# Constant products in TensorE's norm waits: six, one, four and two of them become none

## What is computed

```python
def rms_norm(t, gain):
    t32 = t.astype(jnp.float32)
    y = t32 * lax.rsqrt(jnp.mean(t32 * t32, axis=-1, keepdims=True) + NORM_EPS)
    return (y * gain.astype(jnp.float32)).astype(t.dtype)

# first block
x = (x + gt1 * rms_norm(mix_out, norm_mix_post[l])).astype(x.dtype)
h = rms_norm(x, norm_ffn_pre[l]) * (1.0 + sc2) + sh2
f = jnp.square(jax.nn.relu(h @ w_ff1[l])) @ w_ff2[l]
x = (x + gt2 * rms_norm(f, norm_ffn_post[l])).astype(x.dtype)
# hybrid layer
h = rms_norm_2(x, g_mix)
proj = h @ w_in
...
g = jax.nn.sigmoid(rms_norm_2(x, g_ple_in) @ w_ple_gate)
return x + g * e
```

## Time and profile before

| | |
|---|---|
| median of 3 runs | 3424.12 us (3423.11 to 3424.27) |
| profiled execution | 3424.06 us, span 3422.1 us |
| TensorE products, busy | 3238.1 us, 95% of the span |
| TensorE weight loads, busy | 2564.4 us, 75% |
| VectorE, ScalarE, GpSimd, busy | 1995.4, 1066.0, 1673.5 us |
| granted TensorE clock, mean | 0.98 of full speed |
| moved by DMA | 268.37 MB, mean 78 GB/s |

### The profile page before, as it was taken

How to read it: one execution, slowest core, us unless ns; L and a number is a source line. 1 busy time by engine, 2 the same in 40 slices (tenths; PEclk the granted TensorE clock), 3 DMA queues, 4 the chain that set the end, 5 groups by cost and what they waited for, 6 DMA issues and landing times.

```text
span 3422.1 us, 52681 instructions
## 1 busy us (share of the span) xinstructions
PE 3238.1 (95%) x19342; PEld 2564.4 (75%) x19342; DVE 1995.4 (58%) x2743; ACT 1066.0 (31%) x1986; POOL 1673.5 (49%) x1323
## 2 busy tenths in 40 slices
PE   7988999999999999899999999999989999999999
PEld 4766777777888887577777788877657777787887
DVE  5556677755566556524645666656552735586466
ACT  2142433432111113543443311112551535231112
POOL 3423323225476664144444666655226263566665
PEclk9998999999999999899999999999999999999999
DMA  5431111112233222012122222322012121223232
GB/s 208 154 136 45 45 38 43 40 32 79 91 98 98 96 88 68 26 62 68 56 68 63 86 98 92 98 80 86 31 38 93 44 82 49 81 93 98 92 98 93
DMA packets 71658, 268.37 MB, mean 78 GB/s; under 512 B 7840, under 2 KB 7968, under 8 KB 68384
## 3 DMA queue, kind: packets, MB, share of 16 engines
q1 hardware_dynamic: 69152, 260.73, 23.0%
q10 hardware_dynamic: 2304, 4.83, 0.4%
HBM read 263.44 MB, written 2.10 MB: 78 GB/s over the span
## 4 chain that ended last, share of the span: by engine, by line
PE 77%; DVE 16%; ACT 4%; issue 2%; DMA 1%; POOL 0%; SPq 0%; DVEq 0%; ACTq 0%; POOLq 0%
PE psum_a L574 10%; PE psum_a L578 10%; PE psum_a L577 10%; PE psum_d L574 5%; PE psum_d L578 5%; PE psum_d L577 5%; PE psum_d L637 4%; PE psum_a L729 3%; PE psum_d L832 2%; PE psum_a L600 2%; PE psum_a L603 2%; PE psum_a L604 2%; PE psum_a L759 1%; PE psum_a L763 1%; PE psum_a L762 1%
## 5 line engine op out<-in xcount | busy, mean ns | idle before, releaser
L3306 POOL TENSOR_TENSOR w_lo<-raw,w_hi 128x1024 fp32r<-128x1024 f32 x440 | 1114.4, 2533 | 36.7
L3302 POOL TENSOR_TENSOR mark<-mark 128x1 f32<-128x1 f32 x438 | 104.9, 240 | 1672.4 <-PE psum_a L574 838.1
L574 PE MATMUL psum_a<-h_hi,w_hi 128*128 128x512 f32 x1712 | 676.0, 395 | 0.0
L578 PE MATMUL psum_a<-h_hi,w_lo 128*128 128x512 f32 x1712 | 668.3, 390 | 0.0
L577 PE MATMUL psum_a<-h_lo,w_hi 128*128 128x512 f32 x1712 | 668.0, 390 | 0.0
L3303 POOL TENSOR_SCALAR w_hi<-raw 128x1024 fp32r<-128x1024 f32 x440 | 471.2, 1071 | 33.8 <-DMA raw<-in_weights 33.8
L574 PEld LDWEIGHTS psum_a<-h_hi,w_hi 128*128 128x128 f32 x1712 | 322.7, 189 | 77.7 <-issue 11.2
L577 PEld LDWEIGHTS psum_a<-h_lo,w_hi 128*128 128x128 f32 x1712 | 322.6, 188 | 67.6 <-issue 1.9
L578 PEld LDWEIGHTS psum_a<-h_hi,w_lo 128*128 128x128 f32 x1712 | 322.3, 188 | 67.9
L574 PE MATMUL psum_d<-split,w_hi 128*128 128x512 f32 x848 | 331.1, 390 | 9.6 <-DVE x L3053 6.8
L577 PE MATMUL psum_d<-split,w_hi 128*128 128x512 f32 x848 | 330.0, 389 | 0.0
(11 more groups left out here) (396 smaller groups left out, 5702.1 us busy)
## 6 DMA issues: line engine op xcount, KB each, us to landing
raw<-in_weights SPq DMA_DIRECT2D x440, 512.0 KB, 3.4
plain<-in_ada SPq DMA_DIRECT2D x20, 1024.0 KB, 6.9
arena<-in_ada SPq DMA_DIRECT2D x4, 1024.0 KB, 17.5
x<-in_x SPq DMA_DIRECT2D x1, 2048.0 KB, 12.8
x<-in_x ACTq DMA_DIRECT2D x1, 2048.0 KB, 10.7
out<-x SPq DMA_DIRECT2D x8, 256.0 KB, 3.7
arena<-in_pe ACTq DMA_DIRECT2D x2, 512.0 KB, 4.4
const<-in_const ACTq DMA_DIRECT2D x1, 906.0 KB, 9.3
```

The lines of the kernel that those rows point to most:

```text
L574: m = pe.eng.matmul(dst, wh, hi(t), start=t == 0, stop=False)
L578: m = pe.eng.matmul(dst, wl, hi(t), start=False, stop=t == k - 1)
L3302: eng.tensor_tensor(b.mark[:, 1:2], b.mark[:, 0:1], b.mark[:, 0:1], ALU.add)
L3306: eng.tensor_tensor(lo, b.raw[:, s], hi.bitcast(F32), ALU.subtract).then_inc(sig["w_ready"], 1)
```

## The change

One line of constants. All calls of pe_unused and the loop in pe_norm_direct stay, with zero products each; so does the wait on free_a in pe_unused and the wait on free_d in pe_norm_direct. Every other instruction of every engine stays as it was.

```diff
@@ -668,7 +668,7 @@
         pe.eng.matmul(pe.b.psum["a"][:, n0 % BANKS, 0:2 * P], pe.b.ident, pe.b.const[:, C_MASK4:C_MASK4 + 2 * P], start=True, stop=True)
 
 
-UNUSED = (6, 1, 4, 2)
+UNUSED = (0, 0, 0, 0)
 
 
 def pe_norm(pe, N):
```

## The result

The changed kernel takes 3439.6 us (median of 5), the kernel before 3423.45 us beside it: 16.2 us more, ratio 1.0047 with a 95% interval of 1.0037 to 1.0058. The profiled execution took 3441.41 us, 17.35 more than that of before; it is the longest of the five.

A forecast was written before the change was run, and what follows sets the result against it. TensorE bounds the kernel (77% of the chain), with short waits for norms. Low-clock terms of 4.4, 3.5, 2.3, 1.2 and 3.3 us over five stretches give 14.7, so 3424.1 + 14.7 = 3438.8 us, range 3429 to 3447.

The forecast's parts named there:

- A: 899 to 924 us, pe_norm then pe_norm_direct: spread 0.8, turns 0.4, last spread 0.9, restart 2.3, together 4.4 us slower.
- B: 1273 to 1299 us, pe_norm then pe_norm_direct: spread 0.8, turns 0.4, restart 2.3, together 3.5 us slower.
- C: 2293 to 2306 us, pe_norm alone: sums and spread already at the low clock, so only the restart, 2.3 us slower.
- D: 2350 to 2365 us, pe_norm alone: restart 2.3, less 0.5 already low, less 0.6 for products in the way: 1.2 slower.
- E: 3362 to 3373 us, pe_norm alone: sums +0.9, spread +0.7, restart 2.3, less 0.6: 3.3 us slower.
- restart: Full product stream behind each norm begins at half rate, low for 4.7 us on average: 2.3 us lost each, 1.6 to 2.9.
- waits and turns: Sums, spreads and direct turns ahead of the products: low clock adds up to 0.9 per spread or sums, 0.4 for turns.
- Direct turns: Sums in pe_norm_direct, A and B: 1.66 to 1.75 us a turn at low clock, now 1.757; net +0.4, between -0.8 and +0.7.
- Rival 1: The clock keeps its level in A, turns at 1.51 us, only gains are left: 3419.4 us, chance 0.06.
- Rival 2: Low restarts behind each norm are hidden by VectorE and ScalarE splitting h, only 3.7 us stay: 3427.8 us, chance 0.09.
- Rival 3: Low level costs half its whole length, 67 us more low in the five stretches, 33.5 lost: 3457.6 us, chance 0.03.
- The allowance for the moment: Some twelve later unfilled waits meet the clock's changes at other moments, a microsecond or two each either way, together about 3.

The follow-up runs named there:

- e1: Kernel before without the two constant products of each direct turn, the other constant products kept: 3427.36 against 3422.9 us, +4.5, ratio 1.0014.
- e3: Kernel before without the four constant products behind each spread, the others kept: 3456.16 against 3422.9 us, +33.3, ratio 1.0104.
- e4: Kernel before with one constant product in each direct turn in place of two: 3429.86 against 3422.9 us, +7.0, ratio 1.0027.
- e8: Changed kernel with the two products of each direct turn put back: 3461.04 us against 3423.5 for the kernel before, +37.5, ratio 1.0114.
- e7: Changed kernel with the four products behind each spread put back: 3427.65 us against 3423.5 for the kernel before, +4.2, ratio 1.0015.
- The two shifts: Kernel before with eight, then four, constant products added once ahead of A's norm: 3426.37 against 3423.5 us (+2.9), and 3426.17 against 3422.7 (+3.5).
- e2: Kernel before without the six constant products ahead of the first sums, the others kept: 3427.49 against 3422.9 us, +4.6, ratio 1.0016.

## Why the prediction was right, step by step

**The direction and the mechanism held.** The removed products gave back nothing where they had stood in waits, and the clock fell in the first waits of A and B. The forecast of 3438.8 us stands against 3439.6, +14.7 against +16.2.

**The single terms, from the profiled executions.** A weight load that both kernels have stands later in the changed kernel by what was lost up to there. The lag is 0.0 us ahead of A and 5.4 behind it, 10.1 behind B, 10.2 ahead of C and 13.1 behind it, 14.7 behind D, 13.8 ahead of E and 17.5 behind it. For A the load behind the restart, before and after (931.90 + 5.42 = 937.32):

```profile
931.90 0.19 PEld L603 LDWEIGHTS psum_a<-h_lo,w_hi 128*128 128x128 f32 x1
...
937.32 0.19 PEld L603 LDWEIGHTS psum_a<-h_lo,w_hi 128*128 128x128 f32 x1
```

The first L600 of each stretch divides its loss into waits and turns ahead of it and the restart behind it:

| stretch | waits and turns, forecast | measured | restart, forecast | measured | sum, forecast | measured |
|---|---|---|---|---|---|---|
| A | 2.1 | 2.6 | 2.3 | 2.8 | 4.4 | 5.4 |
| B | 1.2 | 2.1 | 2.3 | 2.6 | 3.5 | 4.7 |
| C | 0 | 0.1 | 2.3 | 2.8 | 2.3 | 2.9 |
| D | -0.6 | -0.4 | 1.8 | 2.0 | 1.2 | 1.6 |
| E | 1.0 | 1.1 | 2.3 | 2.6 | 3.3 | 3.7 |

The sum is 18.3 us where 14.7 were forecast, so every term was too small, the restarts by 1.8 us together and the waits and turns by 1.8. The restart was sized by the mean of five of the old kernel, 4.7 us low; the five that came were low for 6.0, 5.6, 6.0, 5.4 and 5.7. Two of the five that were averaged (3.2 and 3.4 us) were shorter than any that came. In the waits it is above all B: its last spread was taken as low already, and the rest as in A, but 0.9 us more were lost.

**What made up for it.** The span grew by 17.5 us and not by 18.3, because of low stretches outside the norms. The kernel before has one of 3.4 us, among products that run without a gap:

```profile
2397.20:2400.40 3.20, 3.20 (x9) 2.49 (x8) 0.20 (x1) 0.28 (x2) 2.99 (x3) 0.50 0.00 0
```

The changed kernel has 1.00 over the same work (the window from 2405 to 2420 us above), and the lag falls from 14.7 to 13.1 us there. Against it, a low stretch that was 6.8 us long from 2513 on is 10.2 us long in the changed kernel and costs 0.8 us. The start of that work, before and after:

```profile
2510.50:2513.10 2.60, 1.11 (x8) 0.29 (x8) 1.19 (x3) 0.00 (x0) 0.00 (x0) 1.00 0.62 205
...
2523.60:2526.20 2.60, 2.04 (x8) 0.44 (x8) 0.37 (x2) 0.00 (x0) 0.00 (x0) 0.50 0.58 205
```

In sum these later low stretches kept their length, as the forecast's last sign asks, and each cost or gave what stood in it. The forecast had allowed some 3 us for such changes without saying which way. The terms were 3.6 us too small; 0.8 us of that was taken back outside the norms, and the median of the changed kernel lies 1.8 us under its profiled execution. That the forecast of the median came within 0.8 us is therefore in part luck.

**Direct turns.** At the low level 1.66 to 1.72 us a turn were forecast, 1.72 measured; without products the lower clock costs what the removal gives. e1 showed the 1.51 of the high level, and e3, e4 and e8 what the turn would cost with slow products in it, 3.41 and 2.56. Had the change left the two products in the turns, it would have cost more than twice as much.

**Rival 1** (the clock stays, 3419.4) fell with the windows of A. **Rival 2** (the restarts are hidden, 3427.8) fell with the table and with e7: four products behind each spread, which take the restarts away and little else, moved 12.0 of the 16.2 us. **Rival 3** (half of the whole low time, 3457.6) fell with A itself: A was low for 30.7 us and lost 5.4. The rule of the Trainium skill (TensorE: Matmul & The Clock Gate, Terms), that half of the throttled time is lost, holds roughly in these traces for the part of it in which products run without a gap: A's restart was low for 6.0 us and lost 2.8, but A as a whole would be 15 us by that rule, and lost 5.4.

**The allowance for the moment** is the weakest step. The two shifts did not test it. That low stretches come and go without any change to the work is shown by the part ahead of A, which is the same in both kernels. The profiled execution of before is at 0.50 for 6.8 us from 724.6 on; that of the changed kernel is for 3.4 us there, and again at 782.7, where before has 1.00. Before, then after:

```profile
778.00:800.00 22.00, 19.25 (x110) 15.87 (x109) 10.58 (x18) 5.69 (x13) 8.43 (x7) 1.00 0.16 51
...
782.70:786.10 3.40, 3.40 (x12) 2.92 (x13) 1.38 (x2) 0.92 (x3) 1.41 (x3) 0.51 0.02 5
```

So the stretch that vanished at 2397 need not be an effect of the change. What decides which of them come is open.

## What to carry to other kernels

A product without a reader in a wait is worth what the clock is worth behind the wait: price it by the products that follow at half rate, not by the length of the wait. Fill the wait to its end and check in the trace that it is the wait you meant; a product where TensorE doesn't wait costs its own time, and one inside a loop that runs at the low level costs twice its time each turn. A difference of one or two microseconds needs more than one profiled execution, since low stretches elsewhere come and go. Parts of such a filling do not add up: taking all of it away cost 16 us, taking one of its parts away 33.

## What the runs showed of the hardware

- Taking the filling out of the waits behind the spreads put the clock at 0.50 in A for 30.7 us, through the turns with their two constant products (e3). In the kernel before, the same turns run at 1.00 from end to end. With the products behind the spread in place (the kernel before, e2) the turns in A ran at 1.00; without them the clock fell during the second turn (e3) or was low from the start (e8), and did not come back before the products behind A.
- Eight one-column passes took 0.95 to 1.05 us at 1.00 and 1.69 to 1.87 at 0.50, and a single load 0.19 and 0.33 us: at the lower level loads slow down like products.
- The clock fell under one product a turn (e4) as it did under none (e1), within a microsecond of each other, 910.9 against 910.2.
